# A hybrid decoder block on one core: the z-gate and memory-query chunks of the scan groups as 512-column products over two PSUM banks each

## The chip, the cores and the metric

The kernel runs on one core of a Trainium2 chip. The metric is the device time of one execution in microseconds, less is better. The kernel before takes 680.98 us, the median of 3 runs (680.88 to 681.19).

## What is computed

The reference is one layer on 256 tokens of width 1024. Cut to what the change touches:

```
u = rms_norm(h, mix_norm_g);  proj = u @ w_in        # q, k, v, z, xBC, dt, memory q, gates
xbc = silu(causal_dwconv(xbc, ssm_conv_w, ssm_conv_b))
y   = ssd_chunked_scan(xs, dt, a_neg, bm, cm, D)     # 4 groups of 8 heads
v   = y * silu(z);  o_ssm = v * rsqrt(mean(v*v over a group)) * g
o_mem = cross attention of the memory q into 256 memory tokens
...                                                   # attention, merge, output projection
hid = causal_dwconv(rms_norm(h) @ w_ffn_up);  h + (silu(g) * up) @ w_ffn_down
```

## The kernel before, in words

Every float32 product is made of three float32r products: weights and tokens are each split into a high and a low part, and low times low is left out. Weights come in chunks of 256 columns by 1024 rows (8 tiles of 128x256) into three slots of `w_raw`. For each chunk ScalarE copies the high part (`split_hi`, L340), VectorE subtracts the low part (`split_lo`, L344), TensorE multiplies. After a chunk is multiplied its slot's `w_hi` is overwritten by the next one's, so a `split_hi` waits for the chunk before in that slot.

There are two ways to multiply a chunk. `gemm_cols` issues, for each of two halves of 128 columns, 8 times three products of 256 token columns (L385 to L387), into one bank. `gemm_both` (L371) uses that the high and low tokens stand side by side in `tok`: 8 products of 512 columns with `w_hi` (L378) give high times high in the left half of a bank and high times low in the right half; 8 products of 256 columns with `w_lo` (L380) are added on the left. The two halves of the bank must then be summed: ScalarE copies the right halves, VectorE adds the left ones. Before the change this is used for the attention keys and queries and for the late feed-forward chunks.

The input projection of the scan is done in four groups (0 to 3). A group has six chunks: three that go through the convolution (B and C, and two of x), then two of z, then one of memory queries. TensorE's order in a group from 1 on is: three convolution chunks into banks 0, 1, 2; `scan` of the group before into banks 6 and 7 (L706, L707); then `rest_of_group`: two z chunks (banks 0, 1), eight transposes of x (L691, banks 3 and 4), the C times B product (L694 and L695, bank 5), and the memory-query chunk (bank 2). In group 0 there is no scan, and `decay_sums` stands between the halves of its first z chunk.

All engines run orders written out by hand; each waits on counting semaphores. VectorE's order in `group`: convolution, split, `activate` (L1487), ..., `scan_out` (L1461, L1466), the other `activate`s, then `silu_z` (L1492) with a `split_lo` behind it, twice, then the two `x_dt` products (L1516), the masked `cb` (L1521), `split_lo` of slot 2, the large `decay` product (L1525), and `sum_squares`. ScalarE's: for each z chunk tanh straight from PSUM (L1089), `split_hi`, exponents (L1118); then the copy of the memory queries (L1105), `split_hi`, the exponential of `decay` (L1108).

```
def gemm_both(pe, s, banks, both, other=None):
    for j in range(2):
        if other is not None and j:
            pe.wait_ge(*other)
```

At the end of the kernel the last feed-forward steps run the same way in `ffn` on VectorE (`pad_with` L1799, `convolve` L1817, silu L1827, `hid` L1833, low part L1837), and TensorE's last work is `down` of three chunks (`down_part`, `down_end`), which waits for the split weights and for `hid`'s low part.

Of the kernel before, what the change touches and what calls it, by code (L numbers as in the profile page):

```python
# [19 lines left out]
ALU = mybir.AluOpType  # L20
ACT = mybir.ActivationFunctionType
# [42 lines left out]
RW = 2 * CW  # L64
HK = KT // 2
K_BANKS = (0, 1)
V_BANKS, G1_BANKS, OUT_BANKS, H_BANKS = (2, 5), (0, 7), ((2, 3), (6, 7)), (4, 5, 7, 3)
F_BANKS = (0, 1), (2, 3)
WIDE, LOW_KQ = 3, 8
SUM_BANKS, GATE_BANKS = (0, 1), (6, 7)  # L70
Y_PARTS = ((0, 0, 512, 4), (0, 512, 512, 5), (1, 0, 512, 6), (1, 512, 256, 1), (1, 768, 256, 3))
Y_STAT = (6, 7, 8, 9, 0)
# [35 lines left out]
def build(nc, x, mem, w_in, b_gate, w_mem_kv, w_br_attn, w_br_ssm, w_br_mem, w_out, w_ffn_up, w_ffn_down,  # L108
# [4 lines left out]
    def place(name, at, shape, dtype=F32):  # L113
# [160 lines left out]
    y_step, v_ready, squared, sq_step = map(sem, ("y_step", "v_ready", "squared", "sq_step"))  # L274
# [72 lines left out]
    def gemm_cols(pe, r, s, hi, lo, k0=0, banks=None, free=None, start=True, stop=True, tiles=None, between=None):  # L347


        pe.wait_ge(lo_ready[s], r + 2)  # L350
        for b in [s] if free is None else free:
            pe.wait_ge(bank_free[b], r + 1)
        for j in range(2):
            o = ps[:, s, j * T:(j + 1) * T] if banks is None else ps[:, banks[j], 0:T]
            mm = cols_part(pe, s, j, range(KT), o, hi, lo, k0, start, stop, None if j else tiles)
            if between is not None and j == 0:
                between()
        mm.then_inc(gemm_done[s], 1)
# [8 lines left out]
                       start and k == ks[0], stop and k == ks[-1], **kw)  # L367
        return mm

    def gemm_both(pe, s, banks, both, other=None):  # L370


        for j in range(2):
            if other is not None and j:
                pe.wait_ge(*other)
            cuts = [slice(k * CW + j * P, k * CW + (j + 1) * P) for k in range(KT)]
# [90 lines left out]
    def halves(b):  # L467
        return ps[:, b, :].rearrange("p (a n) -> p a n", a=2)
# [12 lines left out]
    with nc.Block() as block:  # L481
# [129 lines left out]
        def _(pe):  # L611
# [71 lines left out]

            def rest_of_group(g, between=None):
                r = 2 * g + 1
                gemm_cols(pe, r, 0, tok_hi, tok_lo, between=between)
                gemm_cols(pe, r, 1, tok_hi, tok_lo)
                pe.wait_ge(conv_done, 3 * g + 3)
                for t in range(NT):
                    for c in range(GT):  # L690
                        mm = pe.transpose(ps[:, 3 + t, c * P:(c + 1) * P], conv_o[:, 2 + c, t * P:(t + 1) * P], ident)  # L691
                mm.then_inc(xg_turned, 1)

                pe.matmul(ps[:, 5, 0:T], conv_o[:, 0, 0:P], conv_o[:, 1, :], start=True, stop=True)  # L694
                pe.matmul(ps[:, 5, T:T + P], conv_o[:, 0, P:T], conv_o[:, 1, P:T], start=True,  # L695
                          stop=True).then_inc(cb_mm, 1)
                gemm_cols(pe, r, 2, tok_hi, tok_lo)

            def scan(n):

# [308 lines left out]
        def _(act):  # L1009
# [44 lines left out]
            def group(g, first=False, last=False):  # L1054
# [31 lines left out]
                for s in range(2):  # L1086
                    act.wait_ge(gemm_done[s], r + 2)
                    act.wait_ge(conv_done, 3 * g + s + 1)
                    act.activation(tanh_a[:, s], halves(s), ACT.Tanh, scale=0.5).then_inc(z_tanh, 1)  # L1089
                    split_hi(act, r + 2, s)  # L1090
                    if first:
                        if s == 0:
                            act.wait_ge(acs_out, 16 * NT)
                            load_acs(0)
                        for t in range(NT) if s else ():
                            exponents(g, t, range(HPG))
                            if t == 0:
# [274 lines left out]
        def _(dve):  # L1372
# [84 lines left out]
            def scan_out(n):  # L1457

                dve.wait_ge(y_mm, n)
                for c in range(GT):  # L1460
                    dve.scalar_tensor_tensor(y_sum[:, c, :], conv_o[:, 2 + c, :],  # L1461
                                             cols_skip[:, bass.ds(GT * n - GT + c, 1)],
                                             ps[:, 6 + c // 2, (c % 2) * T:(c % 2 + 1) * T], ALU.mult,
                                             ALU.add).then_inc(y_step, 1)
                dve.wait_ge(y_step, GT * n)
                dve.scalar_tensor_tensor(v_ssm[:, bass.ds(GT * n - GT, GT), :], z_act[:], 0.5, y_sum[:], ALU.mult,  # L1466
                                         ALU.mult).then_inc(v_ready, 1)


            def group(g, first=False):  # L1470
# [19 lines left out]
                def silu_z(s):  # L1490
                    dve.wait_ge(z_tanh, 2 * g + s + 1)
                    dve.scalar_tensor_tensor(z_act[:, 2 * s:2 * s + 2, :], tanh_a[:, s], 1.0, halves(s), ALU.add,  # L1492
                                             ALU.mult).then_inc(bank_free[s], 1)
                    split_lo(dve, r + 2, s)

                convolve(0)
                split_lo(dve, r + 1, 0)
# [9 lines left out]
                if not first:  # L1507
                    scan_out(g)
                    dve.wait_ge(v_ready, g)
                    activate(1)  # L1510
                activate(2)
                silu_z(0)
                silu_z(1)
                dve.wait_ge(xg_turned, g + 1)
                for t in range(NT):
                    dve.tensor_tensor(x_dt[:, t, :].rearrange("p (h n) -> p h n", n=SHD),  # L1516
                                      ps[:, 3 + t, :].rearrange("p (h n) -> p h n", n=SHD),
                                      dt_s[:, t, bass.ds(HPG * g, HPG)].unsqueeze(2).to_broadcast([P, HPG, SHD]),
                                      ALU.mult).then_inc(xdt_ready, 1)
                dve.wait_ge(cb_mm, g + 1)  # L1520
                dve.tensor_tensor(cb[:], ps[:, 5, 0:3 * P], cb_mask, ALU.mult).then_inc(cb_masked, 1)  # L1521
# [42 lines left out]

            def heads(i, first=False):
                r = RB + i
                dve.wait_ge(low_part, 2 * i + 1)
                dve.tensor_tensor(k_t[:], part_pair(K_BANKS, 0), k_t[:], ALU.add).then_inc(bank_free[0], 1)
                split_lo(dve, r + 1, 0)
                dve.wait_ge(low_part, 2 * i + 2)  # L1570
# [222 lines left out]
            def ffn(f, sa, ra, sb, rb, early, after_gate, after_up, hi=hid_hi, lo=hid_lo, wide=False):  # L1793

                def pad_with(s, r, pad, splits):
                    if wide:
# [176 lines left out]
```

## Time and profile before

| | |
|---|---|
| median of 3 runs | 680.98 us |
| the profiled execution's own time | 681.85 us |
| its span in the trace | 680.1 us |
| busy: TensorE (PE) / its weight loads | 670.1 / 596.2 us |
| busy: VectorE (DVE) / ScalarE (ACT) / GpSimd (POOL) | 500.5 / 386.3 / 16.5 us |
| mean granted TensorE clock | 0.998 |

PE is TensorE, PEld its weight loads, DVE VectorE, ACT ScalarE, SP the engine that starts most transfers. Start times are from the span's start. A row of a timeline gives start, length, engine, line, operation, and in brackets the idle time before it and what ended it; instructions of one line that follow each other are merged, and "x6" counts them. A matmul's row ends later than the next one's start, because they are pipelined: the distance between two starts is what a product costs.

### The profile page before, as it was taken

What the parts mean: (1) busy time and instruction counts of PE and PEld (TensorE: products, weight loads), DVE (VectorE), ACT (ScalarE), POOL (GpSimd) and SP (SyncE); (2) the same over time, 40 slices, a digit from 0 to 9 for tenths busy, and PEclk for the clock granted to TensorE, in tenths of its full rate; (3) what the DMA queues carried; (4) which work ended last, traced back from release to release, by engine and by line L of the source; (5) the groups of instructions that cost most, each with busy time, mean ns of one, the idle gap of its engine ahead of it and who ended that gap; (6) DMA issues with size and microseconds to landing.
All of it is one profiled execution on the core that took longest, in us unless ns stands there. A gap on an engine that the chain in (4) does not pass through costs nothing.

```text
span 680.1 us, 10673 instructions
## 1 busy us (share of the span) xinstructions
PE 670.1 (99%) x4121; PEld 596.2 (88%) x4121; DVE 500.5 (74%) x625; ACT 386.3 (57%) x491; POOL 16.5 (2%) x29
## 2 busy tenths in 40 slices
PE   8999999999999999999999999999999999999996
PEld 6999999999888889999888888888899888888875
DVE  6885979697868666777755655556689877777786
ACT  6558867767655554555533333443567565566662
POOL 0000000000100000000000000000130000000001
PEclk9999999999999999999999999999999999999999
DMA  9875767569285457545566755565445555555621
GB/s 298 241 256 180 247 201 241 165 214 345 71 235 190 151 177 233 167 147 180 158 230 200 233 187 185 187 223 179 161 140 195 186 185 185 190 193 190 198 93 63
DMA packets 99744, 130.92 MB, mean 193 GB/s; under 512 B 5631, under 2 KB 73980, under 8 KB 99068
## 3 DMA queue, kind: packets, MB, share of 16 engines
q1 hardware_dynamic: 98164, 125.27, 57.0%
q10 hardware_dynamic: 1544, 5.16, 2.4%
q8 instruction: 24, 0.39, 0.3%
q14 instruction: 12, 0.10, 0.0%
HBM read 129.31 MB, written 2.68 MB: 194 GB/s over the span
## 4 chain that ended last, share of the span: by engine, by line
PE 83%; DVE 9%; ACT 3%; DMA 2%; issue 2%; DVEq 0%; POOL 0%; POOLq 0%; SPq 0%; ACTq 0%
PE ps L385 20%; PE ps L386 20%; PE ps L387 20%; PE ps L378 11%; PE ps L380 6%; DVE w_lo L344 3%; DVE conv_a L1480 2%; DMA acs_b<-acs_d 1%; PE ps L706 1%; ACT decay L1118 1%; DVE conv_g L1817 1%; DMA x_nat<-x 1%; PE ps L440 1%; PE ps L726 1%; PE ps L743 1%
## 5 line engine op out<-in xcount | busy, mean ns | idle before, releaser
L344 DVE TENSOR_TENSOR w_lo<-w_raw,w_hi 128x2048 fp32r<-128x2048 f32 x107 | 244.7, 2288 | 84.6 <-ACT w_hi L340 84.6
L340 ACT ACTIVATE w_hi<-w_raw 128x2048 fp32r<-128x2048 f32 x107 | 204.4, 1911 | 94.3 <-PE ps L387 92.2
L385 PE MATMUL ps<-tok,w_hi 128*128 128x256 f32 x480 | 137.3, 286 | 0.5 <-DVE tok L1396 0.4
L386 PE MATMUL ps<-tok,w_hi 128*128 128x256 f32 x480 | 135.8, 283 | 0.0
L387 PE MATMUL ps<-tok,w_lo 128*128 128x256 f32 x480 | 135.8, 283 | 0.0
L385 PEld LDWEIGHTS ps<-tok,w_hi 128*128 128x128 f32 x480 | 92.0, 192 | 1.9 <-DVE w_lo L1390 0.8
L386 PEld LDWEIGHTS ps<-tok,w_hi 128*128 128x128 f32 x480 | 92.0, 192 | 0.1
L387 PEld LDWEIGHTS ps<-tok,w_lo 128*128 128x128 f32 x480 | 92.0, 192 | 0.0
L378 PE MATMUL ps<-ftok,w_hi 128*128 128x512 f32 x256 | 63.9, 391 | 0.0
L378 PEld LDWEIGHTS ps<-ftok,w_hi 128*128 128x128 f32 x256 | 46.5, 189 | 8.6
L385 PE MATMUL ps<-w_hi,tok 128*128 128x512 f32 x128 | 50.5, 394 | 0.0
L387 PE MATMUL ps<-w_hi,tok 128*128 128x512 f32 x128 | 49.9, 390 | 0.0
L386 PE MATMUL ps<-w_lo,tok 128*128 128x512 f32 x128 | 49.9, 390 | 0.0
L380 PEld LDWEIGHTS ps<-ftok,w_lo 128*128 128x128 f32 x256 | 34.9, 190 | 2.5
L380 PE MATMUL ps<-ftok,w_lo 128*128 128x256 f32 x256 | 35.7, 282 | 0.0
L378 PE MATMUL ps<-tok,w_hi 128*128 128x512 f32 x128 | 32.6, 397 | 0.0
L1480 DVE SCALAR_TENSOR_TENSOR conv_a<-pad_x,params,conv_a 128x256 f32<-128x256 f32 x72 | 29.5, 480 | 0.2
L387 PEld LDWEIGHTS ps<-w_hi,tok 128*128 128x128 f32 x128 | 24.0, 188 | 5.1
L385 PEld LDWEIGHTS ps<-w_hi,tok 128*128 128x128 f32 x128 | 24.0, 188 | 5.0 <-issue 0.2
L386 PEld LDWEIGHTS ps<-w_lo,tok 128*128 128x128 f32 x128 | 24.1, 188 | 4.8
L385 PE MATMUL ps<-w_hi,hid_hi 128*128 128x512 f32 x72 | 28.1, 391 | 0.0
L386 PE MATMUL ps<-w_lo,hid_hi 128*128 128x512 f32 x72 | 28.1, 391 | 0.0
(286 smaller groups left out, 1205.7 us busy)
## 6 DMA issues: line engine op xcount, KB each, us to landing
w_raw<-w_in SPq DMA_DIRECT2D x94, 512.0 KB, 4.9
w_raw<-w_ffn_up SPq DMA_DIRECT2D x44, 512.0 KB, 4.4
w_raw<-w_ffn_down SPq DMA_DIRECT2D x22, 512.0 KB, 4.0
w_raw<-w_mem_kv SPq DMA_DIRECT2D x16, 512.0 KB, 4.6
w_raw<-w_br_ssm SPq DMA_DIRECT2D x16, 512.0 KB, 4.9
acs_b<-acs_d ACTq DMA_DIRECT2D x4, 1024.0 KB, 6.9
w_raw<-w_br_attn SPq DMA_DIRECT2D x8, 512.0 KB, 4.9
w_raw<-w_br_mem SPq DMA_DIRECT2D x8, 512.0 KB, 4.7
```

The lines of the kernel that those rows point to most:

```text
L340: act.activation(w_hi[:, s, :], w_raw[:, s, :], ACT.Copy).then_inc(hi_ready[s], 1)
L344: dve.tensor_tensor(w_lo[:, s, :], w_raw[:, s, :], w_hi[:, s, :].bitcast(F32), ALU.subtract).then_inc(lo_ready[s], 1)
L378: pe.matmul(ps[:, banks[j], :], w_hi[:, s, w], both[:, k], start=k == 0, stop=False)
L380: mm = pe.matmul(ps[:, banks[j], 0:T], w_lo[:, s, w], both[:, k, 0, :], start=False, stop=k == KT - 1)
L385: pe.matmul(o, a[0], b[0], start=start, stop=False, **kw)
L386: pe.matmul(o, a[0], b[1], start=False, stop=False, **kw)
L387: return pe.matmul(o, a[1], b[0], start=False, stop=stop, **kw)
L440: return pe.transpose(ps[:, bank, o:o + P], src[:, t, k * P:(k + 1) * P], ident)
L706: pe.matmul(o, x_dt[:, 0, h * SHD:(h + 1) * SHD], decay[:, h, 0:T], start=True, stop=False)
L726: mm = pe.matmul(ps[:, 3 + a, P:3 * P], q_t[:, a, P:T], k_t[:, a, :], start=True, stop=True)
L743: pe.matmul(ps[:, bank, a * T:(a + 1) * T], v_t[:, 0, at:at + DH], prob_t[:, a, 0:T], start=True, stop=False)
L1480: dve.scalar_tensor_tensor(conv_a[:, s, j, :], pad_x[:, s, j, tap:tap + T], cols_conv[:, tap, bass.ds(conv_tile(s, j, g), 1)], conv_a[:, s ...
```

## The change

The two z chunks and the memory-query chunk of each group (12 chunks in all) are multiplied by `gemm_both`. z goes to banks (0, 1) and (3, 4), the memory queries to (6, 7), the transposed x to 2 and 5, C times B to bank 7. The second half of the memory-query chunk writes bank 7, from which VectorE reads C times B, so it waits for `cb_masked`. The halves are summed by a ScalarE copy of the right ones and a new VectorE add: `add_z` for z, another for the queries. tanh of z is taken from the sum, in a new place of ScalarE's order (`z_tanh_of`), and `silu_z` works on the sum and no longer frees a bank; `add_z` does. `sum_squares` and the second `silu_z` move ahead of the `decay` product. The counts of `low_part` move up by 12. In the last feed-forward step `split_lo` of slot 2 moves from behind the silu to in front of the `pad_u` add.

```diff
+QM_BANKS, Z_BANKS, XG_BANKS, CB_BANK = (6, 7), ((0, 1), (3, 4)), (2, 5), 7
-WIDE, LOW_KQ = 3, 8
+WIDE, LOW_KQ = 3, 8 + 3 * GROUPS
...
             def rest_of_group(g, between=None):
                 r = 2 * g + 1
-                gemm_cols(pe, r, 0, tok_hi, tok_lo, between=between)
-                gemm_cols(pe, r, 1, tok_hi, tok_lo)
+                for s in range(2):
+                    pe.wait_ge(lo_ready[s], r + 2)
+                    pe.wait_ge(bank_free[s], r + 1)
+                    if s == 0:
+                        pe.wait_ge(bank_free[1], r + 1)
+                    gemm_both(pe, s, Z_BANKS[s], tok, between=None if s else between)
                 pe.wait_ge(conv_done, 3 * g + 3)
...
+                if between is None:
+                    pe.wait_ge(y_step, GT * g)
+                else:
+                    pe.wait_ge(acs_ready, 2)
...
-                gemm_cols(pe, r, 2, tok_hi, tok_lo)
+                pe.wait_ge(lo_ready[2], r + 2)
+                pe.wait_ge(bank_free[2], r + 1)
+                gemm_both(pe, 2, QM_BANKS, tok, (cb_masked, g + 1))
...
                     act.wait_ge(conv_done, 3 * g + s + 1)
-                    act.activation(tanh_a[:, s], halves(s), ACT.Tanh, scale=0.5).then_inc(z_tanh, 1)
+                    act.activation(tanh_a[:, s], part_pair(Z_BANKS[s], 1), ACT.Copy).then_inc(low_part, 1)
                     split_hi(act, r + 2, s)
+                    if s:
+                        z_tanh_of(g, s)
...
                     elif s == 0:
                         exponents(g, 0, range(HPG // 2, HPG))
+                        z_tanh_of(g, 0)
...
-                act.activation(qm[:, bass.ds(2 * g, 2), :], halves(2), ACT.Copy).then_inc(bank_free[2], 1)
+                act.activation(qm[:, bass.ds(2 * g, 2), :], part_pair(QM_BANKS, 1), ACT.Copy).then_inc(low_part, 1)
...
+            def z_tanh_of(g, s):
+
+                act.wait_ge(bank_free[s], 2 * g + 3)
+                act.activation(tanh_a[:, s], z_act[:, 2 * s:2 * s + 2, :], ACT.Tanh, scale=0.5).then_inc(z_tanh, 1)
...
+                def add_z(s):
+                    dve.wait_ge(low_part, 3 * g + s + 1)
+                    dve.tensor_tensor(z_act[:, 2 * s:2 * s + 2, :], part_pair(Z_BANKS[s], 0), tanh_a[:, s],
+                                      ALU.add).then_inc(bank_free[s], 1)
...
                 if not first:
                     scan_out(g)
                     dve.wait_ge(v_ready, g)
+                    add_z(0)
                     activate(1)
+                else:
+                    add_z(0)
                 activate(2)
+                split_lo(dve, r + 2, 0)
                 silu_z(0)
-                silu_z(1)
+                add_z(1)
+                split_lo(dve, r + 2, 1)
                 dve.wait_ge(xg_turned, g + 1)
...
+                silu_z(1)
+                if not first:
+                    sum_squares(g)
+                dve.wait_ge(low_part, 3 * g + 3)
+                queries = qm[:, bass.ds(2 * g, 2), :]
+                dve.tensor_tensor(queries, part_pair(QM_BANKS, 0), queries, ALU.add).then_inc(bank_free[2], 1)
                 split_lo(dve, r + 2, 2)
...
                 convolve(0, pad_g, conv_g, 0)
...
+                for rr, ss in between:
+                    split_lo(dve, rr, ss)
                 pad_with(sb, rb, pad_u, [])
...
-            ffn(F_STEPS - 1, 2, RL - 1, 0, RL, [], [(RL, 2)], [(RL + 1, 0)], end_hi, end_lo, wide=True)
+            ffn(F_STEPS - 1, 2, RL - 1, 0, RL, [], [], [(RL + 1, 0)], end_hi, end_lo, wide=True,
+                between=[(RL, 2)])
```

TensorE behind the z chunks in a group from 1 on (before, then with the change; helper lines are three higher there, and `waits` names the semaphores):

```order
L691 MATMUL ps<-square_c,conv_o 128x128 [waits conv_done]
...
L694 MATMUL ps<-conv_o 128x256
L695 MATMUL ps<-conv_o 128x128
L385 MATMUL ps<-tok,w_hi 128x256 [waits bank_free2,lo_ready2]
L386 MATMUL ps<-tok,w_hi 128x256
L387 MATMUL ps<-tok,w_lo 128x256
```

```order
L698 MATMUL ps<-square_c,conv_o 128x128 [waits conv_done]
...
L705 MATMUL ps<-conv_o 128x256 [waits y_step]
L706 MATMUL ps<-conv_o 128x128
L381 MATMUL ps<-tok,w_hi 128x512 [waits bank_free2,lo_ready2]
L381 MATMUL ps<-tok,w_hi 128x512 x7
L383 MATMUL ps<-tok,w_lo 128x256 x8
L376 REGISTER_ALU
L381 MATMUL ps<-tok,w_hi 128x512 [waits cb_masked]
```

The three products, 16 times over, have become two runs of 8 and 8, and between the runs stands a wait for `cb_masked`, which TensorE did not have.

VectorE in the same group, from the end of `scan_out` to `decay` (before, then with the change):

```order
L1466 SCALAR_TENSOR_TENSOR v_ssm<-z_act,y_sum 128x1024
...
L1487 SCALAR_TENSOR_TENSOR conv_o<-tanh_a,conv_a 128x512 [waits conv_tanh]
...
L1492 SCALAR_TENSOR_TENSOR z_act<-tanh_a,ps 128x512 [waits z_tanh]
...
L344 TENSOR_TENSOR w_lo<-w_raw,w_hi 128x2048 [waits hi_ready0]
L1492 SCALAR_TENSOR_TENSOR z_act<-tanh_a,ps 128x512 [waits z_tanh]
L344 TENSOR_TENSOR w_lo<-w_raw,w_hi 128x2048 [waits hi_ready1]
...
L1516 TENSOR_TENSOR x_dt<-ps,dt_s 128x512
...
L1521 TENSOR_TENSOR cb<-ps,square_c 128x384 [waits cb_mm]
L344 TENSOR_TENSOR w_lo<-w_raw,w_hi 128x2048 [waits hi_ready2]
```

```order
L1515 TENSOR_TENSOR z_act<-ps,tanh_a 128x512 [waits low_part,v_ready]
...
L1510 SCALAR_TENSOR_TENSOR conv_o<-tanh_a,conv_a 128x512 [waits conv_tanh]
...
L345 TENSOR_TENSOR w_lo<-w_raw,w_hi 128x2048 [waits hi_ready0]
...
L1521 SCALAR_TENSOR_TENSOR z_act<-tanh_a,z_act 128x512 [waits z_tanh]
L1515 TENSOR_TENSOR z_act<-ps,tanh_a 128x512 [waits low_part]
L345 TENSOR_TENSOR w_lo<-w_raw,w_hi 128x2048 [waits hi_ready1]
...
L1548 TENSOR_TENSOR x_dt<-ps,dt_s 128x512
...
L1553 TENSOR_TENSOR cb<-ps,square_c 128x384 [waits cb_mm]
```

`cb` stands where it stood, behind the split of slot 1 and the two `x_dt` products; an add has come in front of `conv_o`.

## Rows read from the trace of the kernel before

**Rows 1.** The profile's page: TensorE's and its weight loads' totals, and its granted clock

```profile
PE 670.1 (99%) x4121; PEld 596.2 (88%) x4121; DVE 500.5 (74%) x625; ACT 386.3 (57%) x491; POOL 16.5 (2%) x29
PEclk9999999999999999999999999999999999999999
```

**Rows 2.** Timeline of TensorE, group 2 into group 3 (start, length, engine, line)

```profile
121.78 1.03 PE L691 MATMUL ps<-square_c,conv_o 128*128 128x128 f32 x8
...
123.23 0.36 PE L385 MATMUL ps<-tok,w_hi 128*128 128x256 f32 x1
...
146.42 0.66 PE L706 MATMUL ps<-decay,x_dt 128*64 128x256 f32 x4
...
149.23 0.38 PE L385 MATMUL ps<-tok,w_hi 128*128 128x256 f32 x1
...
160.84 1.03 PE L691 MATMUL ps<-square_c,conv_o 128*128 128x128 f32 x8
```

**Rows 3.** The chain of waits, first keys chunk: its two halves' starts and the next chunk's

```profile
168.28 1.84 PE ps L378 x8
...
173.87 1.84 PE ps L378 x8
```

**Rows 4.** ACT's timeline behind the second z chunk of group 2

```profile
122.07 0.60 ACT L1089 ACTIVATE tanh_a<-ps 128x512 f32<-128x512 f32 x1 [1.76 <-PE ps L387]
122.56 1.91 ACT L340 ACTIVATE w_hi<-w_raw 128x2048 fp32r<-128x2048 f32 x1
```

**Rows 5.** DVE's timeline in group 2

```profile
117.72 1.29 DVE L1487 SCALAR_TENSOR_TENSOR conv_o<-tanh_a,conv_a 128x512 f32<-128x512 f32 x2
...
124.50 2.29 DVE L344 TENSOR_TENSOR w_lo<-w_raw,w_hi 128x2048 fp32r<-128x2048 f32 x1 [1.11 <-ACT w_hi L340]
126.71 1.28 DVE L1516 TENSOR_TENSOR x_dt<-ps,dt_s 128x512 f32<-128x512 f32 x2
127.91 0.55 DVE L1521 TENSOR_TENSOR cb<-ps,square_c 128x384 f32<-128x384 f32 x1
...
134.52 3.36 DVE L1525 TENSOR_TENSOR decay<-decay,cb 128x3072 f32<-128x3072 f32 x1 [0.44 <-ACT decay L1108]
```

**Rows 6.** Group 0: TensorE's transposes, and DVE's masked product behind them

```profile
42.67 1.04 PE L691 MATMUL ps<-square_c,conv_o 128*128 128x128 f32 x8
...
48.72 0.55 DVE L1521 TENSOR_TENSOR cb<-ps,square_c 128x384 f32<-128x384 f32 x1
```

**Rows 7.** Group 1: DVE's last activates, and TensorE's transposes that wait for them

```profile
81.31 1.29 DVE L1487 SCALAR_TENSOR_TENSOR conv_o<-tanh_a,conv_a 128x512 f32<-128x512 f32 x2
...
82.66 1.09 PE L691 MATMUL ps<-square_c,conv_o 128*128 128x128 f32 x8 [0.76 <-DVE conv_o L1487]
```

**Rows 8.** The end of the kernel: timelines of ACT, DVE and TensorE

```profile
656.32 1.90 ACT L340 ACTIVATE w_hi<-w_raw 128x2048 fp32r<-128x2048 f32 x1
...
659.25 0.69 DVE L1799 TENSOR_TENSOR pad_u<-ps,low_u 128x512 f32<-128x512 f32 x1 [1.53 <-ACT low_u L1319]
...
667.25 0.68 DVE L1837 TENSOR_TENSOR end_lo<-hid,end_hi 128x512 fp32r<-128x512 f32 x1
...
661.52 0.39 PE L387 MATMUL ps<-w_hi,hid_lo 128*128 128x512 f32 x1
662.89 0.47 PE L385 MATMUL ps<-w_hi,last_hi 128*128 128x512 f32 x1 [0.98 <-DVE w_lo L344]
663.20 0.40 PE L386 MATMUL ps<-w_lo,last_hi 128*128 128x512 f32 x1
```

**Rows 9.** Stretches at the end: us, busy PE, PEld, DVE, ACT, POOL, then PEclk, DMA share, GB/s

```profile
674.00:675.00 1.00, 0.09 (x1) 0.00 (x0) 1.00 (x3) 0.74 (x5) 0.59 (x2) 1.00 0.00 0
...
676.00:677.00 1.00, 0.00 (x0) 0.00 (x0) 0.66 (x2) 0.67 (x1) 0.23 (x1) 0.89 0.88 328
```

**Rows 10.** The keys' copy and add, by line: lowest, median and highest length in ns

```profile
L1143 ACT ACTIVATE k_t<-ps x4: 576/598/599, 173.9 to 234.2; 128x512 f32<-128x512 f32 x4
...
L1568 DVE TENSOR_TENSOR k_t<-ps,k_t x4: 684/688/692, 177.9 to 238.5; 128x512 f32<-128x512 f32 x4
```

More of the change, by code:

```diff
@@ L273, in build @@
         sem, ("xg_turned", "cb_mm", "cb_masked", "xdt_ready", "y_mm", "z_tanh"))
-    y_step, v_ready, squared, sq_step = map(sem, ("y_step", "v_ready", "squared", "sq_step"))
+    y_step, v_ready, squared, sq_step, z_ready = map(sem, ("y_step", "v_ready", "squared", "sq_step", "z_ready"))
     group_mm, group_var, group_pow, group_kept, rstd_g_in = map(
@@ L368, in cols_part, with gemm_both @@
         return mm
-    def gemm_both(pe, s, banks, both, other=None):
+    def gemm_both(pe, s, banks, both, other=None, between=None):
         for j in range(2):
@@ L375, in gemm_both @@
                 pe.wait_ge(*other)
+            if between is not None and j:
+                between()
             cuts = [slice(k * CW + j * P, k * CW + (j + 1) * P) for k in range(KT)]
@@ L690, in rest_of_group @@
                     for c in range(GT):
-                        mm = pe.transpose(ps[:, 3 + t, c * P:(c + 1) * P], conv_o[:, 2 + c, t * P:(t + 1) * P], ident)
+                        mm = pe.transpose(ps[:, XG_BANKS[t], c * P:(c + 1) * P], conv_o[:, 2 + c, t * P:(t + 1) * P], ident)
                 mm.then_inc(xg_turned, 1)
-                pe.matmul(ps[:, 5, 0:T], conv_o[:, 0, 0:P], conv_o[:, 1, :], start=True, stop=True)
-                pe.matmul(ps[:, 5, T:T + P], conv_o[:, 0, P:T], conv_o[:, 1, P:T], start=True,
+                if between is None:
+                    pe.wait_ge(y_step, GT * g)
+                else:
+                    pe.wait_ge(acs_ready, 2)
+                pe.matmul(ps[:, CB_BANK, 0:T], conv_o[:, 0, 0:P], conv_o[:, 1, :], start=True, stop=True)
+                pe.matmul(ps[:, CB_BANK, T:T + P], conv_o[:, 0, P:T], conv_o[:, 1, P:T], start=True,
                           stop=True).then_inc(cb_mm, 1)
-                gemm_cols(pe, r, 2, tok_hi, tok_lo)
+                pe.wait_ge(lo_ready[2], r + 2)
+                pe.wait_ge(bank_free[2], r + 1)
+                gemm_both(pe, 2, QM_BANKS, tok, (cb_masked, g + 1))
             def scan(n):
@@ L1100, in group @@
                         exponents(g, 0, range(HPG // 2, HPG))
+                        z_tanh_of(g, 0)
                     else:
@@ L1465, in scan_out @@
                 dve.wait_ge(y_step, GT * n)
+                dve.wait_ge(z_ready, 2 * n)
                 dve.scalar_tensor_tensor(v_ssm[:, bass.ds(GT * n - GT, GT), :], z_act[:], 0.5, y_sum[:], ALU.mult,
@@ L1488, in activate @@
                                              ALU.mult).then_inc(conv_done, 1)
+                def add_z(s):
+                    dve.wait_ge(low_part, 3 * g + s + 1)
+                    dve.tensor_tensor(z_act[:, 2 * s:2 * s + 2, :], part_pair(Z_BANKS[s], 0), tanh_a[:, s],
+                                      ALU.add).then_inc(bank_free[s], 1)
                 def silu_z(s):
+                    z = z_act[:, 2 * s:2 * s + 2, :]
                     dve.wait_ge(z_tanh, 2 * g + s + 1)
-                    dve.scalar_tensor_tensor(z_act[:, 2 * s:2 * s + 2, :], tanh_a[:, s], 1.0, halves(s), ALU.add,
-                                             ALU.mult).then_inc(bank_free[s], 1)
-                    split_lo(dve, r + 2, s)
+                    dve.scalar_tensor_tensor(z, tanh_a[:, s], 1.0, z, ALU.add, ALU.mult).then_inc(z_ready, 1)
                 convolve(0)
@@ L1516, in group @@
                     dve.tensor_tensor(x_dt[:, t, :].rearrange("p (h n) -> p h n", n=SHD),
-                                      ps[:, 3 + t, :].rearrange("p (h n) -> p h n", n=SHD),
+                                      ps[:, XG_BANKS[t], :].rearrange("p (h n) -> p h n", n=SHD),
                                       dt_s[:, t, bass.ds(HPG * g, HPG)].unsqueeze(2).to_broadcast([P, HPG, SHD]),
@@ L1520, in group @@
                 dve.wait_ge(cb_mm, g + 1)
-                dve.tensor_tensor(cb[:], ps[:, 5, 0:3 * P], cb_mask, ALU.mult).then_inc(cb_masked, 1)
+                dve.tensor_tensor(cb[:], ps[:, CB_BANK, 0:3 * P], cb_mask, ALU.mult).then_inc(cb_masked, 1)
+                silu_z(1)
[4 more added lines that the diff above has]
+                dve.tensor_tensor(queries, part_pair(QM_BANKS, 0), queries, ALU.add).then_inc(bank_free[2], 1)
                 split_lo(dve, r + 2, 2)
@@ L1526, in group @@
                                   ALU.mult).then_inc(decay_cb, 1)
-                if not first:
-                    sum_squares(g)
             def sum_squares(n):
@@ L1566, in heads @@
                 r = RB + i
-                dve.wait_ge(low_part, 2 * i + 1)
+                dve.wait_ge(low_part, 3 * GROUPS + 2 * i + 1)
                 dve.tensor_tensor(k_t[:], part_pair(K_BANKS, 0), k_t[:], ALU.add).then_inc(bank_free[0], 1)
                 split_lo(dve, r + 1, 0)
-                dve.wait_ge(low_part, 2 * i + 2)
+                dve.wait_ge(low_part, 3 * GROUPS + 2 * i + 2)
                 dve.scalar_tensor_tensor(q_t[:], part_pair(q_banks(i), 0), DH ** -0.5, q_t[:], ALU.mult,
@@ L1791, in scaled_lo, with ffn @@
                                   ALU.subtract).then_inc(h_lo, 1)
-            def ffn(f, sa, ra, sb, rb, early, after_gate, after_up, hi=hid_hi, lo=hid_lo, wide=False):
+            def ffn(f, sa, ra, sb, rb, early, after_gate, after_up, hi=hid_hi, lo=hid_lo, wide=False, between=()):
                 def pad_with(s, r, pad, splits):
```

## The prediction

> **What bounds the kernel.** I read the page's totals first: TensorE is busy 99% of the span, its granted clock is full throughout [rows 1]. So the question is how densely it is fed. Next its timeline in the groups. From the memory-query chunk of group 2 to the scan of group 3 stand four chunks of three products, 146.42 - 123.23 = 23.19 us, 5.80 each; the whole group, from one batch of transposes to the next, takes 39.06 us [rows 2], which is six such chunks (34.8), the scan (149.23 - 146.42 = 2.81) and the transposes with C times B (123.23 - 121.78 = 1.45) and nothing else. TensorE has no idle time in groups 2 and 3: what it is given less it gives back, and any wait put into it is paid in full. The one exception in the groups is group 1, where it waits 0.76 us for VectorE's `conv_o` [rows 7]. Then ScalarE and VectorE behind the second z chunk [rows 4, 5], since the change makes TensorE wait for `cb`, and last the end of the kernel [rows 8].
>
> **Products.** A keys chunk, which is already done by `gemm_both`, takes 173.87 - 168.28 = 5.59 us [rows 3], against 5.80 for three products: 0.21 less. Twelve chunks change: -2.5 us if all of it counts, 0.64 per group. These rows are of the same tokens, weights and clock, so I take them. The Trainium skill, "TensorE: Matmul & The Clock Gate", section "Back-to-back issue gap", gives a product N/2.4 + 2.5 ns, 109 ns for 256 columns and 216 for 512. An estimate by that page is 5.24 us for 48 short products and 5.20 for the mix, 0.04 saved per chunk and 0.5 in all, which would bring my sum 2.0 us higher. The rows disagree with its level (5.80 is 121 ns a product) and its difference.
>
> **The wait for `cb`.** The second half of the memory-query chunk now writes bank 7 and waits until VectorE has read C times B from it. When is that? Before the change TensorE goes on to the transposes at 121.78, and `cb` ends at 127.91 + 0.55 = 128.46 [rows 2, 5], 6.68 us later. The path is fixed: ScalarE reads the z chunk's bank at 122.07, starts the high part at 122.56 [rows 4], VectorE waits for it (1.11 us idle), splits from 124.50, makes two `x_dt` from 126.71, then `cb` [rows 5]. With the change ScalarE's tanh is a copy of the same size (598 ns against 600) [rows 4, 10], the split still stands in front of `x_dt` and `cb`, and the new add (688 ns long) [rows 10] fits in VectorE's idle 1.11 us. So `cb` again ends 6.7 us after the z chunks. TensorE reaches the wait after 1.45 (transposes, C times B) + 2.79 (half of 5.59) = 4.24 us. It stands for 2.44 us, and 0.15 more: the semaphore (VectorE's end at 82.60 to TensorE's start at 82.66 [rows 7]) and a first product that takes 0.31 instead of 0.23 us [rows 8]. I take 2.6 in groups 2 and 3. Queued behind it are only TensorE's own products, and nobody has idle time that gives it back. Net per group -0.64 + 2.6 = +1.95, two groups +3.9.
>
> **Group 0.** Transposes at 42.67, `cb` ends at 49.27 [rows 6], 6.60 later: a wait of 2.5, net +1.85 at its end.
>
> **Group 1.** Here VectorE decides. Its chain comes from the exponents of group 0, which the change does not move, so its activates would start at 81.31 again; `add_z` now stands in front and takes 0.6 (the distance of two such instructions, from 1.29 for two, 0.69 long). So `conv_o` ends at 83.2. TensorE, which was ready at 82.66 - 0.76 = 81.9 [rows 7], comes at 81.9 + 1.85 - 0.42 = 83.3: the wait of group 0 is swallowed but for 0.6. Then VectorE, with no idle time: from 83.1 a split 2.2, silu 0.6, the second `add_z` 0.6, a split 2.2, two `x_dt` 1.2, `cb` 0.55 [rows 5, 7] make 90.45; TensorE is through its first half at 83.3 + 4.24 = 87.5. Wait 2.9 + 0.15 = 3.05. At the end of group 1 TensorE is 0.6 - 0.21 + 3.05 = 3.45 us late (this contains group 0).
>
> **What costs nothing, and what hides it.** `add_z` in groups 2 and 3: the activates end at 119.01, TensorE wants them at 121.78 [rows 2, 5]; 2.8 us cover 0.6 and the 0.42 by which TensorE comes sooner. Without that cover it is 0.6 per group. The queries' add, `silu_z` and `sum_squares` ahead of `decay`: `decay` ends at 137.88, the scan starts at 146.42 [rows 2, 5], 8.5 us for at most 2.6. ScalarE's two further instructions per group (0.6 each) lie in its 1.76 us of idle time before the second z chunk [rows 4] and similar places. The transfers' order and what frees their slots stay as they are.
>
> **The end.** TensorE's products start every 0.23 us; after 661.52 the next comes at 662.89, so 1.14 us are lost on a split, and 0.08 on the restart [rows 8]. The split moves in front of `pad_u`, where VectorE is idle for 1.53 us. It can start when its high part is there, 656.32 + 1.90 = 658.2, and ends at 660.5, before TensorE's 661.75. `pad_u` comes 1.2 later, but the 2.2 behind the silu are gone, less some 0.15 for ScalarE's start of the convolution: `end_lo` ends at about 667.1 instead of 667.9. TensorE wants it at 661.75 + 24 x 0.227 = 667.2. So -1.2 us, with next to no slack; -0.9 if that slack is missing.
>
> **Sum.** 3.45 + 3.9 - 1.2 = +6.15 us. The profiled execution would go from 681.85 to 688.0; the median of the runs lies 0.87 below it: 680.98 + 6.1 = **687.1 us**.
>
> **Rivals.**
> *The clock falls in the wait.* After TensorE's last product, just past 674.0, the clock is still full up to 676, and 0.89 on average in the microsecond after [rows 9], so it fell to 0.5 at 676.8, 2.7 us after the work ended. The waits of 0.76 and 0.98 us left it full. Mine are 2.5 to 2.6, just under, and 3.05 in group 1, just over. At 1.2 GHz instead of 2.4 the second half of the chunk would take up to 2.8 us more: 689.9 for one fall, up to 698 for four. Chance 0.14. The Trainium skill, same page, section "A second HAM failure mode: psum-queue depth-cycling", tells of a kernel in which short idle times between bursts at the change of banks made the clock swing; the trace has no such swing so far.
> *No wait at all, and faster.* If `cb` is masked when TensorE is through the first half, group 0's gain disappears in group 1's wait, which leaves 0.6 - 0.21 - 2 x 0.64 - 1.2 = -2.1: 678.9. It decides at 4.24 us behind the z chunks; `cb` would have to come 2.4 us sooner, about one split. Everything in front of it stays, so 0.04.
> *A second wait.* The added 0.6 us pieces reach TensorE at the transposes of groups 2 and 3 or elsewhere: +0.6 to +2, 688.4. The slack above speaks against it: 0.07.
> *The change doesn't do what it says*: two-bank chunks are no faster here than three products. Then the 2.1 us that count are missing, 689.2; the keys' rows speak against it: 0.03.
>
> **Numbers.** The forecast has 0.72. A measurement of this kernel tells 0.2%, 1.4 us, from no change. Slower by more: all cases but the second, 0.95; faster 0.04; within 0.01. Range: if each wait is 0.3 shorter (VectorE's order has that much play), 685.9; upward the second wait, the missing gain and one fall, 690.0. Outside it stay the faster case and several falls, and some error of my own: 685.7 to 690.0.
>
> **What would show it.** TensorE idle between the halves of the memory-query chunk four times, put down to VectorE's `cb`: 2.4 us, in group 1 2.9; a query chunk of 8.2 us, z chunks of 5.59; a group of 41.0 us; transposes of group 1 at 83.2; no idle time before the product after `down`'s first chunk at the end. Wrong is the core of it if `cb` ends less than 4.3 us behind the z chunks, and the size if the clock of a wait's slice is under full.

## The result, and the profile after

The changed kernel takes **689.68 us** (median; runs from 688.11 to 690.79), the kernel before 680.93 (680.85 to 681.19) beside it: a ratio of 1.0124, interval 1.0113 to 1.0136. It is 8.8 us slower. I had forecast 687.1, slower, in a range of 685.7 to 690.0: sign and range held and the wait came as forecast, the size was 2.6 us short.

| | before | after |
|---|---|---|
| profiled execution, us | 681.85 | 689.22 |
| TensorE busy, us and share | 670.1, 99% | 670.6, 98% |
| TensorE waits for `cb` | none | 8.8 us in 4 |
| granted clock, mean | 0.998 | 0.995 |
| group 2 to group 3, us | 39.06 [rows 2] | 41.09 |

The page's totals and granted clock and one of its groups, to be held against [rows 1]. TensorE has 192 instructions fewer, twelve chunks with 16 fewer each. The idle time in front of `gemm_both`'s 512-column products (L381) is new, and the last slice of the clock is the kernel's end:

```profile
PE 670.6 (98%) x3929; PEld 587.6 (85%) x3929; DVE 508.3 (74%) x637; ACT 391.3 (57%) x499; POOL 16.5 (2%) x29
PEclk9999999999999999999999999999999999999998
L381 PE MATMUL ps<-tok,w_hi 128*128 128x512 f32 x320 | 83.6, 404 | 8.8 <-DVE cb L1553 8.8
```

TensorE's waits (line waited at, releaser; us in total, times, longest). Four waits of 2.2 us, one per group; the 1.0 at L437 is the wait that was there before:

```profile
PE ps L381 <- DVE cb L1553: 8.8, 4, 2.2
PE ps L437 <- DVE zero_s L1395: 1.0, 1, 1.0
```

TensorE's timeline from the transposes of group 2 to those of group 3, which answers to [rows 2] (x2 and x6 are cut by the edge of the view; each of these runs has 8 products):

```profile
125.90 1.04 PE L698 MATMUL ps<-square_c,conv_o 128*128 128x128 f32 x8
...
132.62 0.74 PE L381 MATMUL ps<-tok,w_hi 128*128 128x512 f32 x2 [2.23 <-DVE cb L1553]
...
135.54 0.28 PE L388 MATMUL ps<-tok,w_hi 128*128 128x256 f32 x1
...
155.71 1.65 PE L381 MATMUL ps<-tok,w_hi 128*128 128x512 f32 x6
...
166.99 1.04 PE L698 MATMUL ps<-square_c,conv_o 128*128 128x128 f32 x8
```

The whole group takes 166.99 - 125.90 = 41.09 us, 2.03 more than before. Two z chunks take 166.99 - 155.71 = 11.28 us, where [rows 2] give 160.84 - 149.23 = 11.61: 0.16 less per chunk, not 0.21. The second half of the query chunk starts at 132.62.

Who releases it: ScalarE, then VectorE in the same group, answering to [rows 4, 5]:

```profile
126.18 0.60 ACT L1102 ACTIVATE tanh_a<-ps 128x512 f32<-128x512 f32 x1 [1.06 <-PE ps L383]
126.68 1.90 ACT L341 ACTIVATE w_hi<-w_raw 128x2048 fp32r<-128x2048 f32 x1
```

```profile
126.81 0.69 DVE L1515 TENSOR_TENSOR z_act<-ps,tanh_a 128x512 f32<-128x512 f32 x1 [0.74 <-ACT tanh_a L1102]
128.61 2.29 DVE L345 TENSOR_TENSOR w_lo<-w_raw,w_hi 128x2048 fp32r<-128x2048 f32 x1 [1.11 <-ACT w_hi L341]
130.82 1.28 DVE L1548 TENSOR_TENSOR x_dt<-ps,dt_s 128x512 f32<-128x512 f32 x2
132.02 0.55 DVE L1553 TENSOR_TENSOR cb<-ps,square_c 128x384 f32<-128x384 f32 x1
```

`cb` ends at 132.57, 6.67 us behind the transposes' start. The order is the one of [rows 5]: copy, high part, low part, two `x_dt`, `cb`. The new add lies in time in which VectorE waited anyway.

Group 0 holds what I had given a chance of 0.14. TensorE's timeline, then the stretches around its wait (us, busy PE, PEld, DVE, ACT, POOL, granted clock, DMA share, GB/s):

```profile
48.88 3.69 PE L381 MATMUL ps<-tok,w_hi 128*128 128x512 f32 x8 [2.15 <-DVE cb L1553]
52.40 1.12 PE L383 MATMUL ps<-tok,w_lo 128*128 128x256 f32 x8
53.36 0.28 PE L388 MATMUL ps<-tok,w_hi 128*128 128x256 f32 x1
```

```profile
48.00:49.00 1.00, 0.12 (x1) 0.13 (x1) 1.00 (x3) 0.68 (x2) 0.00 (x0) 0.97 1.09 384
49.00:52.00 3.00, 3.00 (x7) 2.33 (x8) 0.42 (x1) 3.00 (x9) 0.00 (x0) 0.50 1.10 350
52.00:53.00 1.00, 1.00 (x8) 0.93 (x6) 0.00 (x0) 1.00 (x5) 0.00 (x0) 0.82 1.14 406
```

The clock is full until about 48.94 (0.97 of that microsecond), half (1.2 of 2.4 GHz) until about 52.36, then full again. It fell just behind TensorE's restart at 48.88, so nearly all of the second half ran at half clock until 52.36: that half takes 53.36 - 48.88 = 4.48 us. The other three groups have the same wait, and there the clock stays full.

Last the end of the kernel, TensorE and VectorE, answering to [rows 8]:

```profile
675.38 0.39 PE L390 MATMUL ps<-w_hi,last_lo 128*128 128x512 f32 x1
675.66 0.50 PE L388 MATMUL ps<-w_hi,end_hi 128*128 128x512 f32 x1
676.00 0.39 PE L389 MATMUL ps<-w_lo,end_hi 128*128 128x512 f32 x1
```

```profile
674.93 0.68 DVE L1874 TENSOR_TENSOR end_lo<-hid,end_hi 128x512 fp32r<-128x512 f32 x1
```

The idle 1.14 us on the split are gone. In their place `end_lo` ends at 675.61, just when TensorE wants it (675.38 + 0.23): TensorE starts 0.05 us late, and its first product takes 0.11 more.

### The profile page after: what moved, and what is told of

Read it like the earlier page. It is cut to its first block, busy times and chain, and to the rows that moved or that the text cites. A ratio compares the mean times of both kernels' runs of the same rounds, so it can differ in the third digit from the quotient of the medians.

```text
span 687.4 us, 10327 instructions
## 1 busy us (share of the span) xinstructions
PE 670.6 (98%) x3929; PEld 587.6 (85%) x3929; DVE 508.3 (74%) x637; ACT 391.3 (57%) x499; POOL 16.5 (2%) x29
## 4 chain that ended last, share of the span: by engine, by line
PE 89%; DVE 7%; issue 1%; ACT 1%; DMA 1%; POOL 0%; DVEq 0%; POOLq 0%; SPq 0%; ACTq 0%
PE ps L388 19%; PE ps L389 19%; PE ps L390 19%; PE ps L381 18%; PE ps L383 9%; DVE w_lo L345 2%; PE ps L719 1%; DVE conv_a L1503 1%; ACT w_hi L341 1%; DVE x_dt L1548 1%; DMA x_nat<-x 1%; DVE conv_g L1852 1%; PE ps L720 1%; PE ps L443 1%; PE ps L739 1%
## 5 line engine op out<-in xcount | busy, mean ns | idle before, releaser
L381 PE MATMUL ps<-tok,w_hi 128*128 128x512 f32 x320 | 83.6, 404 | 8.8 <-DVE cb L1553 8.8
L388 PE MATMUL ps<-tok,w_hi 128*128 128x256 f32 x288 | 82.3, 286 | 0.5 <-DVE tok L1418 0.4
L389 PE MATMUL ps<-tok,w_hi 128*128 128x256 f32 x288 | 81.5, 283 | 0.0
L390 PE MATMUL ps<-tok,w_lo 128*128 128x256 f32 x288 | 81.5, 283 | 0.0
L381 PEld LDWEIGHTS ps<-tok,w_hi 128*128 128x128 f32 x320 | 58.6, 192 | 21.1 <-DVE cb L1553 9.6
L381 PE MATMUL ps<-ftok,w_hi 128*128 128x512 f32 x256 | 63.9, 391 | 0.0
L388 PEld LDWEIGHTS ps<-tok,w_hi 128*128 128x128 f32 x288 | 55.2, 192 | 1.2 <-DVE w_lo L1412 0.8
L389 PEld LDWEIGHTS ps<-tok,w_hi 128*128 128x128 f32 x288 | 55.3, 192 | 0.1
L390 PEld LDWEIGHTS ps<-tok,w_lo 128*128 128x128 f32 x288 | 55.2, 192 | 0.0
L381 PEld LDWEIGHTS ps<-ftok,w_hi 128*128 128x128 f32 x256 | 46.5, 189 | 8.6
L383 PEld LDWEIGHTS ps<-tok,w_lo 128*128 128x128 f32 x320 | 43.8, 190 | 3.3
L383 PE MATMUL ps<-tok,w_lo 128*128 128x256 f32 x320 | 44.6, 282 | 0.0
```

What stands on the lines that cost most here:

```text
L388: pe.matmul(o, a[0], b[0], start=start, stop=False, **kw)
L389: pe.matmul(o, a[0], b[1], start=False, stop=False, **kw)
L390: return pe.matmul(o, a[1], b[0], start=False, stop=stop, **kw)
```

## The experiments

Two theories. **A:** the 8.8 us are the wait for `cb` in bank 7, four times 2.2 us and the restart, and its size is what stands ahead of `cb` on VectorE. **B:** some of the loss is not the wait itself but TensorE's clock falling in it. Rivals to both: two-bank chunks save nothing; the end saves nothing.

### C times B in another bank

```
-QM_BANKS, Z_BANKS, XG_BANKS, CB_BANK = (6, 7), ((0, 1), (3, 4)), (2, 5), 7
+QM_BANKS, Z_BANKS, XG_BANKS, CB_BANK = (6, 7), ((0, 1), (3, 4)), (2, 5), 0
+                pe.wait_ge(bank_free[0], r + 2)       # ahead of C times B
-                gemm_both(pe, 2, QM_BANKS, tok, (cb_masked, g + 1))
+                gemm_both(pe, 2, QM_BANKS, tok)
+                pe.wait_ge(cb_masked, g)              # head of the next group, and of the keys
```

> The changed kernel with C times B in bank 0 instead of bank 7, so that the second half of the memory-query chunk waits for nothing; the next chunk that writes bank 0 (7.0 us behind the z chunks) waits for cb_masked instead, which comes 6.7 us behind them. My theory (the wait for cb is the whole loss, the products and the end gain): no idle time of TensorE between the halves, no fall of the clock, 678 to 679 us, 2 to 3 below the kernel before. Rival (the added adds and copies delay other things, the wait is only where it shows): 684 or more, with TensorE idle elsewhere in the groups.

Measured: 679.28 us (678.58 to 681.22, 11 runs), ratio 0.9978, interval 0.9969 to 0.9987. No wait for `cb` is left. TensorE in group 2:

```profile
121.63 2.10 PE L381 MATMUL ps<-tok,w_hi 128*128 128x512 f32 x8
123.56 1.11 PE L383 MATMUL ps<-tok,w_lo 128*128 128x256 f32 x8
124.51 2.00 PE L381 MATMUL ps<-tok,w_hi 128*128 128x512 f32 x8
126.35 1.12 PE L383 MATMUL ps<-tok,w_lo 128*128 128x256 f32 x8
127.31 0.28 PE L388 MATMUL ps<-tok,w_hi 128*128 128x256 f32 x1
```

The query chunk takes 127.31 - 121.63 = 5.68 us; before the change it took 129.06 - 123.23 = 5.83 (the timeline of [rows 2], where the next chunk starts at 129.06). So that two-bank chunks save nothing falls. The deal of the banks alone, which lets the query chunk write the bank that `cb` is read from, costs all of the 8.8 us and 1.6 more: with `cb` in bank 0 the kernel is 10.4 us faster than the changed one.

### `cb` and `x_dt` ahead of the split

```
                 add_z(1)
-                split_lo(dve, r + 2, 1)
+                (the wait for cb_mm, and cb)
                 (the wait for xg_turned, and the two x_dt)
-                (the wait for cb_mm, and cb)
+                split_lo(dve, r + 2, 1)
                 silu_z(1)
```

> The changed kernel with banks and waits as they are, but VectorE masks C times B and makes the two x_dt before the split of slot 1 instead of behind it: cb ends some 2.4 us behind the z chunks, TensorE asks for it at 4.24. My theory: no wait, 678 to 679 us, the same as with cb in bank 0. Rival (the split of slot 1, now 1.8 us later, is what the next group waits for): idle time before the next group's second chunk, 681 or more.

Measured: 679.10 us (678.84 to 679.27, 6 runs), ratio 0.9969, interval 0.9957 to 0.9982. Bank 7 is shared as in the changed kernel, and the wait for `cb` is gone all the same, so it is VectorE's order that sets it. What is left of TensorE's waits in the groups is the one for `conv_o` in group 1:

```profile
PE ps L698 <- DVE conv_o L1510: 0.9, 1, 0.9
```

### One piece fewer in front of `cb`, and one more

```
                 split_lo(dve, r + 2, 1)
+                (cb)                          # first kernel: cb ahead of x_dt
                 (the two x_dt)
-                (cb)
```

```
                 split_lo(dve, r + 2, 1)
+                silu_z(1)                     # second kernel: silu ahead of x_dt and cb
                 (the two x_dt, cb)
-                silu_z(1)
```

> The changed kernel with VectorE's masked cb in front of the two x_dt (1.2 us) instead of behind them: each wait of TensorE is 1.2 us shorter, about 1.2 us long. If waits cost their length and the clock falls only behind long ones: no fall, 687.5 (the sum without falls) - 4 x 1.2 = 682.7 us, spread under 1 us. If the clock falls behind short waits too: 684 to 688 with the spread of the changed kernel.

> The changed kernel with the second silu_z (0.6 us) in front of x_dt and cb: each wait is 0.6 us longer, about 3.0 us. The waits alone: 687.5 + 2.4 = 689.9 us. If longer waits make a fall of the clock more frequent (1.7 us each by the profile of the changed kernel, where it stood at half for 3.4 us): 693 to 697 us, several falls in the profile. Rival (whether it falls hangs on the place in time, not on the length): 691 to 693.

Measured: 683.19 us (683.18 to 683.97, 5 runs), ratio 1.0035, interval 1.0021 to 1.0048, and 694.59 us (691.59 to 698.64, 5 runs), ratio 1.0184, interval 1.0165 to 1.0202. TensorE's waits, first of the shorter, then of the longer:

```profile
PE ps L381 <- DVE cb L1547: 4.2, 4, 1.1
```

```profile
PE ps L381 <- DVE cb L1554: 11.2, 4, 2.8
```

The wait moves as VectorE's pieces say: 1.1 shorter without the two `x_dt` (1.2), 0.6 longer with a silu. The time of the shorter one is that of the wait: from the transposes of group 2 to those of group 3 it takes 162.15 - 122.27 = 39.88 us, 1.30 more than a kernel without the wait (38.58, below). The time of the longer one is not: four times 0.6 us are 2.4, and its median is 4.9 above that of the changed kernel. Its profiled execution is the slowest of its runs, 698.64 us. TensorE in group 2 of it, the stretches around, and its transposes of groups 2 and 3:

```profile
136.01 3.78 PE L381 MATMUL ps<-tok,w_hi 128*128 128x512 f32 x8 [2.83 <-DVE cb L1554]
```

```profile
134.00:135.00 1.00, 0.00 (x0) 0.00 (x0) 1.00 (x3) 1.00 (x4) 0.00 (x0) 1.00 0.19 12
135.00:136.00 1.00, 0.00 (x0) 0.00 (x0) 1.00 (x3) 0.17 (x1) 0.00 (x0) 0.60 0.78 124
136.00:142.00 6.00, 5.99 (x20) 5.22 (x21) 0.98 (x2) 0.36 (x1) 0.00 (x0) 0.50 0.43 152
142.00:143.00 1.00, 1.00 (x10) 1.00 (x10) 0.62 (x1) 1.00 (x2) 0.00 (x0) 0.98 0.00 0
```

```profile
128.69 1.04 PE L698 MATMUL ps<-square_c,conv_o 128*128 128x128 f32 x8
173.08 1.04 PE L698 MATMUL ps<-square_c,conv_o 128*128 128x128 f32 x8
```

The clock fell at about 135.2, within the wait, and came back at about 142.0: 6.8 us at half clock. In this execution it fell in all four groups (mean 0.984); in the others the means were 0.991 to 0.995. In groups 0 and 1 it fell only when TensorE was at work again, about 0.3 and 1.4 us behind the restart, and came back after 3.4 us. The fall of group 1, whose restart is at 92.81:

```profile
94.00:95.00 1.00, 1.00 (x5) 0.78 (x4) 0.00 (x0) 0.00 (x0) 0.00 (x0) 0.62 1.08 384
```

In groups 2 and 3 it fell within the wait and came back after 6.8 us. The two kinds differ in price. With the longer wait a group should take 41.09 + 0.6 = 41.7 us. From group 2 to 3 it takes 173.08 - 128.69 = 44.39, 2.7 more, and so does the rest behind it; from 0 to 1 and from 1 to 2 it takes 43.2, 1.5 more each. Together 8.4 us: 698.64 less these is 690.2, and that is the 687.85 of the next kernel, whose clock stays full, and the four times 0.6. With waits of 1.1 us the clock fell in no group of the profile. The Trainium skill, "TensorE: Matmul & The Clock Gate", section "A second HAM failure mode: psum-queue depth-cycling", tells of a kernel in which short idle times between bursts make the clock swing; these rows agree, and add the lengths: behind idle times of 2.2 us it fell in one group of four, behind 2.8 us in all four, behind 1.1 us in none.

### The wait filled with other products

```
+            def fill():
+                z = zero_s[:].bitcast(mybir.dt.bfloat16)
+                for _ in range(10):
+                    pe.matmul(ps[:, 0, :]..., z, z..., start=True, stop=True)
...
-            if other is not None and j:
-                pe.wait_ge(*other)
             if between is not None and j:
                 between()
+            if other is not None and j:
+                pe.wait_ge(*other)
...
-                gemm_both(pe, 2, QM_BANKS, tok, (cb_masked, g + 1))
+                gemm_both(pe, 2, QM_BANKS, tok, (cb_masked, g + 1), between=fill)
```

Ten products of zeros into bank 0, read by nobody, stand ahead of the wait.

> The changed kernel with ten 512-column products of zeros (bf16, about 0.22 us each, into bank 0, which is free then) between the halves, before the wait for cb, four times. The wait is as long as before, but TensorE works in it. If a fall of the clock is what the runs over 686.7 pay: granted clock full in all groups, 686.5 to 687.2 us, with a spread under 1 us between runs. Rival (the spread and the extra 3 us have another cause): the same 688 to 691 us as the changed kernel, or more by what the products add.

Measured: 687.85 us (687.68 to 688.08, 4 runs), ratio 1.0100, interval 1.0084 to 1.0115. The stretches of group 0 again:

```profile
48.00:50.00 2.00, 2.00 (x9) 1.10 (x8) 1.50 (x3) 1.24 (x4) 0.00 (x0) 1.00 1.09 366
50.00:53.00 3.00, 3.00 (x23) 2.82 (x22) 0.00 (x0) 3.00 (x10) 0.00 (x0) 1.00 1.16 371
```

TensorE gets to its second half no sooner (48.95, against 48.88) but goes through it in 2.92 us at full clock instead of 4.48: the fall cost 1.56 us. 1.8 us are gained against the changed kernel, and the runs lie within 0.4 us of each other instead of 2.7. The clock is full in the other groups' waits too. This shows B, and splits the loss: 687.85 - 680.93 = 6.9 us are wait and edits, 1.8 are the clock. The four runs of the changed kernel fit: 688.11 us at a mean clock of 0.997, 689.22 and 690.15 at 0.995, 690.79 at 0.993.

### The last edit alone, on the kernel before

```
+                for rr, ss in between:
+                    split_lo(dve, rr, ss)
                 pad_with(sb, rb, pad_u, [])
...
-            ffn(F_STEPS - 1, 2, RL - 1, 0, RL, [], [(RL, 2)], [(RL + 1, 0)], end_hi, end_lo, wide=True)
+            ffn(F_STEPS - 1, 2, RL - 1, 0, RL, [], [], [(RL + 1, 0)], end_hi, end_lo, wide=True,
+                between=[(RL, 2)])
```

> The kernel before with only the last edit: the split of slot 2 in the last feed-forward step ahead of the pad_u add. My theory: TensorE's wait at the end (1.1 us) goes, 679.8 us, 1.1 to 1.2 below the kernel before. Rival (end_lo comes later and TensorE waits for it instead): within 0.3 us of the kernel before.

Measured: 679.85 us (679.69 to 682.24, 11 runs), ratio 0.9990, interval 0.9981 to 0.9999: 1.1 us less. In the same profile TensorE's transposes of group 1, for [rows 7]:

```profile
81.71 1.04 PE L691 MATMUL ps<-square_c,conv_o 128*128 128x128 f32 x8
```

No idle time stands in front of them. Nothing in the groups differs between this kernel and the one before, so the 0.76 us wait for `conv_o` in [rows 7] belonged to that one execution, which was also 0.9 us over its median. What differed is a transfer: ScalarE's first exponent of group 0 waits for `acs_b`, in the kernel before and then in this one

```profile
49.73 0.51 ACT L1118 ACTIVATE decay<-acs_b,acs_s 128x256 f32<-128x256 f32 x1 [4.45 <-DMA acs_b<-acs_d]
```

```profile
48.43 0.51 ACT L1118 ACTIVATE decay<-acs_b,acs_s 128x256 f32<-128x256 f32 x1 [3.19 <-DMA acs_b<-acs_d]
```

In the kernel before it came 1.30 us later, and VectorE's activates of group 1 start 81.31 - 80.02 = 1.29 us later with it. In the profiles of all the other kernels this wait is 2.2 to 3.2 us.

### The activates ahead of the first add, with `cb` early

```
                 if not first:
                     scan_out(g)
                     dve.wait_ge(v_ready, g)
-                    add_z(0)
                     activate(1)
-                else:
-                    add_z(0)
                 activate(2)
+                add_z(0)
```

This stands on top of the kernel with `cb` and `x_dt` ahead of the split.

> The version with cb and x_dt ahead of the split of slot 1 (679.1 us), and add_z of the first z chunk moved behind the two activates, so that conv_o is not 0.6 us later than before the change. In that version's profile TensorE waits 0.95 us for conv_o in group 1. If that wait is in most runs: 678.5 us. If it is only in runs whose transfer of acs_b comes late: 679.1, the same.

Measured: **678.65 us** (678.62 to 678.72, 5 runs), ratio 0.9965, interval 0.9951 to 0.9978, the fastest of all, 2.2 us under the kernel before. The wait for `conv_o`, then the first product behind the query chunk in groups 1 and 2:

```profile
PE ps L698 <- DVE conv_o L1510: 0.2, 1, 0.2
```

```profile
88.84 0.28 PE L388 MATMUL ps<-tok,w_hi 128*128 128x256 f32 x1
...
127.42 0.28 PE L388 MATMUL ps<-tok,w_hi 128*128 128x256 f32 x1
```

A group without any wait takes 127.42 - 88.84 = 38.58 us, 0.48 less than the 39.06 of [rows 2]. In the changed kernel the same stretch runs from 94.44 to 135.54, 41.10: one wait for `cb` costs 2.52 us. Group 1 itself still stops TensorE for a moment. Its transposes and its query chunk take 88.84 - 81.46 = 7.38 us, those of group 2 127.42 - 120.30 = 7.12:

```profile
85.32 0.55 DVE L1544 TENSOR_TENSOR cb<-ps,square_c 128x384 f32<-128x384 f32 x1
```

```profile
85.93 2.14 PE L381 MATMUL ps<-tok,w_hi 128*128 128x512 f32 x8
```

Here `cb` ends at 85.87, just when TensorE is through the first half, and the second half starts behind it.

### The changed kernel again

No edit.

> The changed kernel once more, for the spread of its runs and the number of falls in another profile. My theory: waits and edits give 687.5 us without a fall and each fall adds up to 1.7, so the runs lie between 687.5 and 691, with a median near 689.7. Rival (one constant extra of 2.2 us in every run): a spread under 0.5 us.

Measured: 689.49 us (689.30 to 691.94, 4 runs), ratio 1.0136, interval 1.0117 to 1.0154. The profile shows the same four waits, and the same single fall in group 0:

```profile
PE ps L381 <- DVE cb L1553: 8.8, 4, 2.2
```

```profile
49.02 1.53 PE L381 MATMUL ps<-tok,w_hi 128*128 128x512 f32 x3 [2.16 <-DVE cb L1553]
```

```profile
49.00:52.00 3.00, 2.98 (x7) 2.37 (x8) 0.56 (x1) 3.00 (x9) 0.00 (x0) 0.53 1.10 345
```

0.53 over three microseconds puts the fall at about 49.2: again behind the restart, by some 0.15 us.

## Why the prediction was right or wrong

**The wait for `cb`: right.** It came where it was forecast, four times, released by `cb`, which ended 6.67 us behind the z chunks (forecast 6.7). It costs 2.5 us with its restart in groups 1 and 2 (2.6 in group 2 in the forecast) and 2.4 in group 0 (2.5), where the kernel with the filled wait takes 83.32 - 42.32 = 41.00 us to the next transposes against 38.58. Moving `cb` or its bank away takes all of it away, as two experiments show.

**Products: mis-sized.** The term was 0.21 us per chunk; it is 0.16 (0.48 per group, 1.9 us in all instead of 2.5). The 5.80 was a mean over four chunks, and two of them stand next to products of another shape, where a chunk is about 0.1 longer (5.83 behind C times B, 5.85 before the scan). Between such places a chunk of three products takes 134.81 - 129.06 = 5.75, and the keys' 5.59 should have been held against this. The 0.1 is paid after the change as well: the first half of the query chunk is 0.08 longer than the second (2.88 and 2.80 in the kernel with the other bank), and a z chunk takes 5.64 on average, 5.69 behind the scan. The estimate by the Trainium skill, "TensorE: Matmul & The Clock Gate", section "Back-to-back issue gap", 0.04 per chunk, was further off: the trace does not agree with it.

**Group 1: the step that failed.** "The wait of group 0 is swallowed but for 0.6" rested on TensorE idling 0.76 us for `conv_o` in the one profiled execution, and I then took the result off the median, where that idle time mostly is not. That idle time came from one late transfer, as the kernel with the last edit alone shows. So the swallowing was worth nothing, and group 0 costs its full net, 2.42 - 0.48 = 1.9. VectorE was not the bound there: `conv_o` and TensorE's transposes in group 1 of the changed kernel are

```profile
80.90 1.28 DVE L1510 SCALAR_TENSOR_TENSOR conv_o<-tanh_a,conv_a 128x512 f32<-128x512 f32 x2
```

```profile
84.81 1.03 PE L698 MATMUL ps<-square_c,conv_o 128*128 128x128 f32 x8
```

`conv_o` is done at 82.2, 2.6 us before TensorE wants it. 1.5 of these are the fall of the clock in group 0; in the kernel with the filled wait, where it did not fall, they are 1.2 (82.1 and 83.32). The wait for `cb` in this group is 2.23 us like that in group 2, not 2.9. The two errors partly cancel: I had 3.45 us for groups 0 and 1, and by the measured terms they are 2.42 + 2.50 - 2 x 0.48 = 4.0.

**The end: right, between its two cases.** -1.1 us alone on the kernel before, where I had -1.2, and -0.9 without slack. The slack of 0.1 us before `end_lo` was missing, but that costs 0.16.

**What was to cost nothing did.** No wait of TensorE for an add, a silu or `decay` shows in groups 2 and 3. In group 1 the add ahead of the activates counts once the wait for `cb` is gone: 0.9 us for `conv_o`, and 0.2 with the add behind them.

**The clock: a rival that came true.** Four waits (9.8), products (-1.9) and the end (-1.1) make +6.8, 687.7 us; the kernel with the filled wait measures 687.85 and the fastest run of the changed kernel 688.11. The median is 1.8 above the filled one, and the fall in group 0 cost 1.56. I had given one fall 0.14, since in [rows 9] the clock fell 2.7 us after TensorE's last work and my waits were 2.5 to 2.6, "just under". Behind this stood the idea that TensorE keeps its clock if it is back in less than 2.7 us, and that was the error. Here the last product ended at 46.73, TensorE was back at 48.88, and the clock fell at 48.94, 2.2 us behind that product and with TensorE at work; in group 1 of the longer kernel it fell 1.4 us behind the restart. One row at the end of a kernel, without a restart, was too little for a bound that decides 2 us in each group. That the range held is owed to this rival: its upper bound is the time with one fall, the median lies 0.3 us under it, and two of the four runs lie above.

**The terms close.** On the 679.85 us of the kernel with the last edit alone, the products' -1.9 and four waits of 1.3 make 683.2, and 683.19 was measured. With waits of 2.5 and 2.4 they make 687.8, against 687.85 with the filled wait: 0.75 of the 2.6 us by which the forecast was short are these terms, the rest is the clock. With no wait for `cb` they would make 678.0, and the three kernels without it measure 678.65 to 679.28. In the fastest of these the missing part is in its profile: 0.40 us in front of the transposes of group 1 (81.46 - 42.48 = 38.98 instead of 38.58), and 0.26 in that group's transposes and query chunk. So once the wait is gone, VectorE in group 1 is what TensorE runs into.

**What stays open.** Why the clock fell in group 0 in both profiles of the changed kernel and in none of the other three groups, whose waits are as long, isn't settled, nor why the longer waits lost it for 3.4 us in two groups and for 6.8 in two.

## What to carry to other kernels

When banks are dealt anew, ask for each bank who reads it last and what stands ahead of that reader on its engine; here one split of 2.2 us and two products (1.2) ahead of a read of 0.55 us cost 2.5 us per group, five times what the three denser chunks of a group gave. Put the small read that frees a bank first and the long conversion behind it. If TensorE must stand for some two microseconds or more, look at the granted clock behind the wait and not only in it. Check a wait found in one profiled execution against a second before you let it absorb anything. And when two ways to multiply are compared, take both times from chunks that stand between chunks of their own kind.

## What the runs showed of the hardware

TensorE's clock fell behind waits of 2.2 us in one group of four, the same one in two profiles, and behind waits of 2.8 us in four of four; waits of 1.1 us lost it in none. Of these six falls four came only when TensorE was at work again, 0.06 to 1.4 us behind its restart, and each of them lasted 3.4 us and cost 1.5 to 1.6. The two that came within the wait, 2.0 us behind the last product, lasted 6.8 us and cost 2.7 each. At the end of the kernel before, with no restart, the clock fell 2.7 us behind the last product [rows 9]. Products of zeros in the wait kept the clock full, and did not delay what came behind.
